# A two-block transformer layer on one core: an eleventh weight buffer, the gate projection moved ahead of the chunk products, and half of the expert loads issued from ScalarE

## The reference, cut to what matters

```python
def second_block(x, mem, ...):
    h = x + _mixer(...)            # differential attention and gated linear attention (GLA), chunks of 64
    h = h + _cross_attention(...)  # queries from h, keys and values from mem_2, 4 heads of 256
    h = h + _hier_moe(...)         # group of 4, then the best 2 of 8 experts in it; 32 experts in all

def expert_block(args):            # for each expert
    hid = jax.nn.silu(xb @ w_gate[e]) * (xb @ w_up[e])   # 1024 -> 512
    return hid @ w_down[e]                               # 512 -> 1024
```

## Time and profile before

| | us |
|---|---|
| median of 3 runs | 1137.18 (1136.93 to 1137.8) |
| profiled execution, its own time | 1140.0 |
| its span, first to last instruction | 1137.7 |
| PE busy | 931.5 (82% of the span) |
| DVE, POOL, ACT busy | 403.1, 243.2, 170.2 |
| q1, the DMA queue with nearly all the bytes (289 MB) | 64.4% of 16 engines' span |

### The profile page before, as it was taken

How to read it: one execution, slowest core, us unless ns; L and a number is a source line. 1 busy time by engine, 2 the same in 40 slices (tenths; PEclk the granted TensorE clock), 3 DMA queues, 4 the chain that set the end, 5 groups by cost and what they waited for, 6 DMA issues and landing times.

```text
span 1137.7 us, 12449 instructions
## 1 busy us (share of the span) xinstructions
PE 931.5 (82%) x5006; PEld 585.4 (51%) x5006; DVE 403.1 (35%) x984; ACT 170.2 (15%) x370; POOL 243.2 (21%) x368
## 2 busy tenths in 40 slices
PE   7999999999999899699999999665656566574837
PEld 3775487789999778575544554221221212131312
DVE  5537834752234827655545524110010101010101
ACT  2113232530001022022312312000000000000000
POOL 4444132043844849630000000000000000000000
PEclk9999999999999999899999999887787878697879
DMA  7636232233545255234228358999999999999997
GB/s 278 199 116 219 96 126 75 75 104 126 195 169 185 77 189 182 74 138 154 78 74 318 131 215 357 429 428 427 429 426 428 427 428 427 430 427 428 428 421 277
DMA packets 64312, 290.38 MB, mean 255 GB/s; under 512 B 9015, under 2 KB 11902, under 8 KB 52222
## 3 DMA queue, kind: packets, MB, share of 16 engines
q1 hardware_dynamic: 63966, 289.04, 64.4%
q10 hardware_dynamic: 288, 0.52, 0.1%
HBM read 288.51 MB, written 1.05 MB: 255 GB/s over the span
## 4 chain that ended last, share of the span: by engine, by line
PE 61%; DMA 27%; DVE 6%; ACT 2%; SPq 2%; issue 1%; ACTq 0%; DVEq 0%
PE ACC L520 11%; PE ACC L661 10%; PE ACC L535 8%; PE AUX L1050 7%; PE ACC L658 7%; DMA ring<-in_w_e_gate_dram 5%; DMA ring<-in_w_e_down_dram 5%; PE ACC L559 5%; DMA SQE<-in_w_e_up_dram 3%; DMA BIG<-in_w_e_up_dram 3%; DMA PJ<-in_w_e_up_dram 3%; DMA PJ<-in_w_e_down_dram 3%; DMA BIG<-in_w_e_gate_dram 3%; PE AUX L1086 2%; PE ACC L942 2%; DMA SQE<-in_w_e_gate_dram 2%
## 5 line engine op out<-in xcount | busy, mean ns | idle before, releaser
L1282 POOL TENSOR_TENSOR ring<-ring 128x256 f32<-128x256 f32 x272 | 200.5, 767 | 190.2 <-PE ACC L661 75.6
L1050 PE MATMUL AUX<-ring,R 128*32 128x512 f32 x416 | 115.9, 721 | 55.0 <-DMA BIG<-in_w_e_up_dram 20.3
L535 PE MATMUL ACC<-BIG,ring 128*128 128x256 f32 (+1 forms) x464 | 106.2, 382 | 0.0
L535 PEld LDWEIGHTS ACC<-BIG,ring 128*128 128x128 f32 (+1 forms) x464 | 84.6, 187 | 15.6 <-issue 3.6
L2282 DVE SCALAR_TENSOR_TENSOR R<-R,AUX 128x512 f32<-128x512 f32 x8 | 5.5, 688 | 233.8 <-ACT R L1660 233.8
L1050 PE MATMUL AUX<-R 128*32 128x512 f32 x112 | 62.9, 726 | 23.3 <-DMA ring<-in_w_e_gate_dram 13.1
L1050 PE MATMUL AUX<-BIG,R 128*32 128x512 f32 x192 | 54.9, 736 | 28.8 <-DMA PJ<-in_w_e_up_dram 21.1
L1050 PEld LDWEIGHTS AUX<-ring,R 128*32 128x32 f32 x416 | 28.6, 129 | 94.7 <-issue 94.7
L520 PE MATMUL ACC<-ring,BIG 128*128 128x512 f32 (+2 forms) x192 | 75.9, 554 | 0.0
L1050 PE MATMUL AUX<-PJ,R 128*32 128x512 f32 x192 | 53.7, 722 | 17.6 <-DMA ring<-in_w_e_up_dram 10.5
L1086 PE MATMUL AUX<-ring,BIG 128*32 128x512 f32 x192 | 52.3, 705 | 13.8 <-DMA BIG<-in_w_e_down_dram 7.4
(11 more groups left out here) (345 smaller groups left out, 1425.0 us busy)
## 6 DMA issues: line engine op xcount, KB each, us to landing
ring<-in_w_in_dram SPq DMA_DIRECT2D x20, 2048.0 KB, 7.8
ring<-in_w_e_gate_dram SPq DMA_DIRECT2D x14, 2048.0 KB, 27.7
ring<-in_w_e_up_dram SPq DMA_DIRECT2D x12, 2048.0 KB, 29.8
ring<-in_w_e_down_dram SPq DMA_DIRECT2D x10, 2048.0 KB, 29.4
BIG<-in_w_e_up_dram SPq DMA_DIRECT2D x8, 2048.0 KB, 32.5
PJ<-in_w_e_gate_dram SPq DMA_DIRECT2D x6, 2048.0 KB, 26.6
BIG<-in_w_e_down_dram SPq DMA_DIRECT2D x6, 2048.0 KB, 29.0
PJ<-in_w_e_down_dram SPq DMA_DIRECT2D x6, 2048.0 KB, 35.2
```

Source lines behind the costliest of these rows:

```text
L535: mm = nc.tensor.matmul(bank[0:m, j * S:(j + 1) * S], w[:, i, a + j * P:a + j * P + m], rhs[:, i, :], start=(i == 0), stop=(i == k - 1))
L1050: mm = nc.tensor.matmul(bank[r, :], M_xt[:, k, r], w[e][:, k, :], start=(k == 0), stop=(k == KD - 1))
L1282: ins = g.tensor_tensor(out[:, k, :], a[:, k, :], b[:, k, :], op)
```

## The change

1. `STREAM` is 11. The new buffer, load 4, is `R12`, which is `R1` and `R2` made one tensor; SP issues it when the turned keys and queries of the cross attention (`xk`, `xq`) are out of it. All later buffers move on by one. To make room, `M_xt` goes to `R4`, `M_o`, `M_gated` and `M_hid` to `GB`, the turned rows for the router (`X3T`) to `BIG2`, the routing scratch over the mask tensors, `OUT` to `PJ`. The `BIG2` load (9) now waits for `("router", 1)`.
2. From load 13 on, the odd ones (39 of them, up to 91) are issued by ACT, behind the tanh, the up products or the down copies of the group that frees the buffer.
3. In the mixer `gg` comes right after `ckv1` on PE, then `kend`, intra, the turns, and the states move into `dv`, after its fourth matmul. On DVE, `gv` is combined whole before `norm_heads`, `ckv1` first thing in its `apply`, then `gg`, `kend`, intra. ACT's tanh of `gg` moves ahead of its drains.
4. Before the mixer, `row_sums` for `mem_2` moves between the two halves of block one's result, and the `rsqrt` for `mem_2` behind `ckv0`; the sums of squares of `X3` get their own columns (76, 77), so that nothing has to wait for those at 64.

```diff
-STREAM = 10
+STREAM = 11
-        stream = [slots[4], slots[5]] + [... ("wcq0", "wcq1")] + spare[0:2] + [
+        stream = [slots[4], slots[5]] + [... ("wcq0", "wcq1")] + [R12[:, :]] + spare[0:2] + [
+        FIRST_BY_ACT, LAST_WHOLE = STREAM + 2, 3 * GROUP * GROUPS - GROUP
+        def by_act(n):
+            return n % 2 == 1 and FIRST_BY_ACT <= n < LAST_WHOLE
# PE
             project_blocks("ckv1", R2T, T_mem2, mem2_sums)
+            project_blocks("gg", XT3, T_x, x1_sums)
             pe.wait_ge(gla_products, 1)
             pe.wait_ge(gla_padded, 1)
+            bank, full = aux(3, "kend")
...
-            project_blocks("gg", XT3, T_x, x1_sums)
-            wait_drained(pe, "kend")
...
-            project("dv", XT3, between=finish_gla)
+            project("dv", XT3, between=finish_gla, after=lambda done, total: make_states() if done == 4 else None)
# SP
-                        if n in (STREAM, STREAM + 1):
+                        if n in (STREAM, STREAM + 1) or by_act(n):
                             continue
                         elif n == 4:
+                            for t in range(TT):
+                                for h in range(2):
+                                    wait_full(sp, ("xk", t, h))
+                                    wait_full(sp, ("xq", t, h))
+                        elif n == 5:
...
                         elif n == 9:
+                            wait_full(sp, ("router", 1))
+                        elif n == 10:
                             wait_full(sp, ("x3", 1, 1))
                             sp.wait_ge(rows_scaled, 2)
# ACT
+            def load_after(g, kind):
+                for e in range(GROUP):
+                    n = load_no(g, kind, e) + STREAM
+                    if by_act(n):
+                        act.dma_start(stream[n % STREAM], weights_of(n)).then_inc(moe_landed[n % STREAM], 16)
             for g in range(GROUPS):
                 act.wait_ge(moe_gate, g + 1)
                 a_.activation(M_gated, AUX[2][:, :], ACT.Tanh, scale=0.5).then_inc(moe_tanh, 1)
+                load_after(g, 0)
+                act.wait_ge(moe_up, g + 1)
+                load_after(g, 1)
                 act.wait_ge(moe_picks_turned, g + 1)
...
+                load_after(g, 2)
# DVE
                 if h == 0:
-                    dve.wait_ge(rows_squared, 4)
-                    rsqrt(2, SMALL[:, 64:66], SMALL[:, 78:80]).then_inc(mem2_scaled, 1)
-            row_sums(T_mem2, quarters(R2T), mem2_sums)
-            norm_rows(3, X3, ZTv, 5)
+                    row_sums(T_mem2, quarters(R2T), mem2_sums)
+            norm_rows(3, X3, ZTv, 5, col=76)
...
-            combine("gv", by_rows(GV), range(1))
+            combine("gv", by_rows(GV))
             def apply_d():
-                combine("gv", by_rows(GV), range(1, 2))
+                combine("ckv1", by_rows(R1v, 512))
...
-            combine("ckv1", by_rows(R1v, 512))
+            combine("gg", by_rows(GG))
             link(v.memset(ATT, 0.0))
```

More of the change, by code:

```diff
@@ L84, in two_block_layer @@
         ident = sb("ident", P)
-        causal = sb("causal", S)
-        past = sb("past", P)
-        future = sb("future", P)
+        MASKS = sb("MASKS", S + 3 * P)
+        causal, past, future, ones = MASKS[:, 0:S], MASKS[:, S:S + P], MASKS[:, S + P:S + 2 * P], MASKS[:, S + 2 * P:]
         before = sb("before", P, BF16)
@@ L831, in _ @@
             project_blocks("ckv1", R2T, T_mem2, mem2_sums)
+            project_blocks("gg", XT3, T_x, x1_sums)
             pe.wait_ge(gla_products, 1)
             pe.wait_ge(gla_padded, 1)
+            bank, full = aux(3, "kend")
+            for t in range(TT):
+                for h in range(2):
+                    mm = nc.tensor.transpose(bank[:, (2 * t + h) * P:(2 * t + h + 1) * P], KE[:, h, t * P:(t + 1) * P],
+                                             ident[:, :])
+            mm.then_inc(full, 1)
             for t in range(TT):
@@ L846, in _, with make_states @@
                 turn(2 + t, ("dk", t))
[L847 to L852, removed]
-            project_blocks("gg", XT3, T_x, x1_sums)
-            wait_drained(pe, "kend")
[L855 to L861, removed]
+            def make_states():
+                wait_drained(pe, "kend")
+                wait_drained(pe, "gv")
+                for c in range(3):
+                    bank, full = aux(c, ("state", c))
+                    for h in range(2):
+                        mm = nc.tensor.matmul(bank[:, h * 256:(h + 1) * 256], KEN[:, c % 2, 2 * (c // 2) + h, :],
+                                              GV[:, c // 2, h * 256:(h + 1) * 256], start=True, stop=True)
+                    mm.then_inc(full, 1)
             def finish_gla():
@@ L954, in score_experts @@
                         wait_drained(pe, ("x3", t, i // 4))
[L955 removed]
+                    mm = nc.tensor.matmul(bank[:, 0:36], X3T[:, i, t * P:(t + 1) * P], WR3[:, i, :],
                                           start=(i == 0), stop=(i == KD - 1))
@@ L1168, in _ @@
             for g in range(GROUPS):
-                for kind, w in enumerate((WG, WU, WD)):
+                for kind in range(3):
                     for e in range(GROUP):
                         n = load_no(g, kind, e)
-                        if n in (STREAM, STREAM + 1):
+                        if n in (STREAM, STREAM + 1) or by_act(n):
                             continue
@@ L1381, in link, with square_rows @@
                 act.wait_ge(act_steps, steps[0])
-            def square_rows(n, src, junk, ready, tiles=range(TT)):
+            def square_rows(n, src, junk, ready, tiles=range(TT), col=64):
                 for r in ready:
@@ L1584, in _ @@
             scale_mem2("ckv1", R1v, 512)
+            act.wait_ge(gla_products, 1)
+            act.wait_ge(gla_padded, 1)
+            wait_drained(act, "gg")
+            a_.activation(R3[:, 0:1024], GG.rearrange("p t n -> p (t n)"), ACT.Tanh, scale=0.5).then_inc(tanh_ready, 1)
             act.wait_ge(pads_cleared, 5)
@@ L2103, in _ @@
             norm_heads(SQ[:, :], 32, 64, apply_d, 2)
-            combine("ckv1", by_rows(R1v, 512))
+            combine("gg", by_rows(GG))
             link(v.memset(ATT, 0.0))
+            bank = wait_full(dve, "kend")
+            kb_ = bank[:, :].rearrange("p (n d) -> p n d", n=4)
+            v.tensor_copy(KEN[0:64, 0, :, :], kb_[0:64])
+            v.tensor_copy(KEN[64:128, 1, :, :], kb_[64:128]).then_inc(free_sem("kend"), 1)
             for t in range(TT):
@@ L2112, in _ @@
                                   pb[:, 1]).then_inc(free_sem(("intra", t)), 1)
-            bank = wait_full(dve, "kend")
-            kb_ = bank[:, :].rearrange("p (n d) -> p n d", n=4)
-            v.tensor_copy(KEN[0:64, 0, :, :], kb_[0:64])
-            v.tensor_copy(KEN[64:128, 1, :, :], kb_[64:128]).then_inc(free_sem("kend"), 1)
-            combine("gg", by_rows(GG))
             for c in range(3):
```

67 lines of the change are left out of this document (33 added, 34 removed).

## The result

The changed kernel takes 1123.47 us (median of 4 runs, 1122.32 to 1124.0), the kernel before, run beside it, 1137.06 (4 runs, 1136.47 to 1137.8). The ratio is 0.9879, 95% interval 0.9862 to 0.9896: faster by 13.6 us. The interval is 11.8 to 15.7 us; the forecast was 17.4 us less, 1119.8, and the range 1113 to 1128. The profiled execution of after took 1124.0 (span 1122.2), that of before 1140.0 (span 1137.7): 16.0 between the two, 15.5 between their spans.

What follows compares the result with a forecast made beforehand. DMA rate bounds the last 430 us, PE the front: the end is the full-queue moment plus bytes left at 428 GB/s. Front 12.5 plus buffer 4.9 is 17.4 us less, median 1119.8, range 1113 to 1128.

Steps and rivals of the forecast that it cites:

- wait before `ckv1`: Mixer: PE's wait for DVE's part 2 of `gv` goes whole, 8.7 us less.
- clock behind it: Mixer: without the wait PE's clock need not fall to half, so `ckv1` is 2.8 us shorter.
- wait before `kend`, clock of `gg`: Mixer: PE's wait for a PSUM bank drained by ACT goes, 2.4 us, and `gg` behind it shortens by 1.0.
- POOL late for `gg`: Mixer: POOL's additions at 0.80 us each finish late, PE waits within `gg`, taking back 3.3 us.
- ahead of the mixer: Before the mixer: DVE's root for x1 starts earlier, shortening PE's 2.88 us wait; 0.9 us less, between 0 and 4.
- eleventh buffer: Its load falls while DMA engines idle, leaving 88 loads instead of 89 at the full queue: 4.9 us less.
- The median of the runs is 2.8 less, and I take the same difference off it: Whole kernel: profiled 1140.0 against median 1137.18; the same 2.8 us was assumed between profile and median after the change.
- Rival 1: Expert stage: two queues fill each other's gaps, rate rises to 434 GB/s, 6 us more gained, 1113.8; chance 0.12.
- rival 4: Expert stage: two queues cost rate; at 406 GB/s 23.2 us more, slower at 1143.0; chance 0.04.
- Rival 3: Change-over to the full queue: a hole eats the extra buffer's lead, 12.5 us gained alone, 1124.7; chance 0.12.
- Rival 2: Front: POOL or DVE slow when packed closer, or the clock drops again; mixer gives 7, 1125.3; chance 0.14.
- in this stretch neither a faster PE nor an earlier issue counts: Expert stage, last 430 us: DMA engines are the bound, each new load standing behind six others.

Runs made afterwards that it cites:

- e7: Kernel before with the eleventh buffer and the moved scratch tensors only, all loads on SP, mixer as before: 1133.18 us, ratio 0.996.
- e3: Changed kernel with ten buffers instead of eleven, `R12` left idle: 1129.38 us, ratio to the kernel before 0.9927.
- e2: Changed kernel with every load issued by SP again: 1124.13 us, ratio to the kernel before 0.9888.
- e8: Changed kernel with every load from 13 on issued by ACT: 1124.56 us, ratio to the kernel before 0.9897.
- e1: Kernel before with only the new order in and ahead of the mixer (parts 3 and 4), ten buffers, all loads on SP: 1129.16 us, ratio 0.9927.
- e4: Changed kernel with POOL's weight sums of `gg` ahead of its three GLA products: 1121.21 us, ratio to the kernel before 0.9854.
- e12: Changed kernel with POOL's `gg` sums first, then the `KE` product, and 9 idle matmuls in the wait for x1: 1120.72 us, ratio to before 0.9858.
- e5: Kernel before, unedited, run again for a second profiled execution: 1136.98 us, ratio 1.0002.
- e10: Kernel before with 12 idle matmuls on PE inside the 2.88 us wait ahead of the turning of x1: 1136.9 us, ratio 1.0.
- e11: Changed kernel with 9 idle matmuls on PE inside the 2.2 us wait ahead of the turning of x1: 1123.55 us, ratio to before 0.9881.
- e6: Kernel before with one edit, DVE combining `gv` whole ahead of `norm_heads`: 1140.48 us, ratio 1.0028.
- e9: Kernel before with 38 idle bf16 matmuls of zeros on PE in the long wait ahead of `ckv1`: 1136.18 us, ratio 0.9989.

## Why the prediction was right, and where it was not

The mechanism was the forecast one: the end is the moment of the full queue plus the bytes left at 428 GB/s, the front moves that moment, and the buffer the bytes. Its terms, from profile to profile:

| term | forecast | measured | from |
|---|---|---|---|
| wait before `ckv1` | 8.7 | 8.7 | no wait in after; part 2 of `gv` on DVE at 458.07, PE asks at 458.80 |
| clock behind it | 2.8 | 2.7 | 14.99 to 12.25 |
| wait before `kend`, clock of `gg` | 3.4 | 3.4 | no wait; the first 3.69 for 16, as at full clock |
| POOL late for `gg` | -3.3 | -5.7 | 471.00 to 488.94 is 17.9, a block is 12.2 |
| ahead of the mixer | 0.9 | 1.0 | `ckv1` begins at 458.80, PE left `gv` at 459.80 |
| rest of the front | 0 | 0.5 | what is left of 10.6 at the router |
| front | 12.5 | 10.6 | router 687.43 to 676.86 |
| eleventh buffer | 4.9 | 4.7 | landing 15.3 earlier, less 10.6; e7 4.5, e3 5.5 |
| issues on ACT | 0 | 0 | no difference shown (e2 1.0, e8 2.0 us slower than after, interval some 2.5); 427 to 428 GB/s |

Two steps failed in size. The first makes up the way from the forecast 17.4 to the 15.3 between the landings (16.0 between the profiled times, 0.5 of it outside the spans), the second the way from there to the 13.6 between the medians.

**POOL's durations.** The step "`gg`'s steps at 475.9, 479.1, 482.3 and 485.5" took 0.80 us an addition from the earlier trace rows. POOL began `gg`'s sums at 471.57, 1.1 earlier than I had it, and PE began `gg` 1.0 earlier; but the twelve additions up to the fifth product took 12.0 us instead of 9.6. In the same stretch DVE's eight scalings of `dq` and `dk` took 8.6 us; in the profile of before, where POOL had nothing to do until 474.96, they took 5.1:

```profile
465.90 1.28 DVE L1751 TENSOR_TENSOR PJ<-PJ,RS 128x512 f32<-128x512 f32 x2
...
468.68 1.29 DVE L1751 TENSOR_TENSOR PJ<-PJ,RS 128x512 f32<-128x512 f32 x2
470.00 2.50 DVE L1757 TENSOR_TENSOR PJ<-PJ,GB 128x512 f32<-128x512 f32 x4
```

The row behind the 0.80 was a mean of two prices. In the profile of before, too, an addition takes 0.73 us as a rule and 1.17 beside the six masked products of the earlier trace rows, which read two operands from SBUF as the scalings do; beside `combine`, whose operations read an accumulator in PSUM, it stays at 0.73:

```profile
L1282 POOL TENSOR_TENSOR ring<-ring x8: 725/728/732, 443.0 to 448.0; 128x256 f32<-128x256 f32 x8
L1282 POOL TENSOR_TENSOR ring<-ring x6: 1052/1173/1258, 448.8 to 454.5; 128x256 f32<-128x256 f32 x6
```

So the price of the two side by side was in the trace of before, and the mean hid it. The new order put the scalings beside the first eight additions of `gg`, and those are what PE waited for: 2.4 us more than the 3.3 of the sum. e1 shows 1.56 and 2.53 us of wait without the buffer and without ACT's issues; e4 and e12 show that the time hangs on POOL's order.

**The step from the profile to the median.** "The median of the runs is 2.8 less, and I take the same difference off it" was wrong. After's profile is only 0.5 above its median, e1's 0.15 below. The profiled execution of before was a long one of its kind, and so was e5's. It carried stretches at half clock that e10's does not have: 1.7 us behind the wait for x1 (2.38 + 4.92 against 1.97 + 3.62), 1.0 in `ckv1` (14.99 against 14.02), and 1.5 from `kend` to the states (14.1 against 12.6). That is 4.2 us, and e10's profiled execution took 1135.8, 4.2 less than before's. After's profile carries the first of the three too, so the pair should differ by 16.0 - 4.2 + 1.7 = 13.5 without them; the medians differ by 13.6. So of the sum's terms "2.8" for the clock behind the wait and "1.0" for `gg` behind `kend`, some 1 us each is there in some executions only. That the median execution of before lacks these stretches is argued, not shown: no profile fell on an unedited execution at 1137, and the match of 13.5 may be luck, for the pair e10 and e11 gives 12.4. What decides whether the clock falls behind a wait of 2 to 3 us also stays open; it fell in before, e5, e7 and after, and not in e1 to e4, e6, e8 and e9, behind waits of 2.2 to 2.9 us.

Rival 1 and rival 4 were about the rate of two queues: it is 427 to 428 GB/s over 100 us in after and in e2, well below rival 1's 434, so both fell. Rival 3 fell with e3 and e7, though its 1124.7 is the nearest number to the result. Rival 2, the mixer gives 7, has its mechanism in the trace: POOL and DVE did get slower when packed closer, at a price of 2.4 us; in the median the mixer gave 8.3, nearer to rival 2 than to the 12.5 of the sum. The change-over cost 0.3 us: load 9 went out at 678.8, at the end of the router product, but the share was full only from 680.6 and not "from about 674". The prediction's "in this stretch neither a faster PE nor an earlier issue counts" held in before and after, but in e4's and e8's profiles PE made the end 1.2 to 1.7 us later. Of what else was priced at nothing, the states' DVE work under four matmuls of `dv` cost nothing that shows.

## What to carry to other kernels

Where transfers end the kernel, two things count first: when the queue is full for good, and how many bytes are still out then; one more buffer was worth one load's time because its load fell into an idle stretch. Look again at the last few us after each gain: in e4 and e8 the products on PE, and no longer the last transfers, were the end. When a reordering puts two engines' work side by side, do not price it with a mean over a long row: split the row by what the other engine did, and take the part in which it did the same. A difference read off one profile should be checked against the spread of the runs: if the profiled execution stands above its median, look for half-clock stretches behind short waits before passing the gain on to the median.

## What the runs showed of the hardware that was not expected

- DVE and POOL side by side slow each other, by what they read: POOL's 128x256 additions take 0.73 us, and 1.17 beside DVE's products of two SBUF operands (before and after); DVE's eight 128x512 scalings take 5.1 us alone and 8.6 beside POOL. Beside the operations of `combine`, which read one operand from PSUM, POOL's additions stay at 0.73.
- The granted clock fell to 0.5 after PE's idle 8.66 us in the long wait, and not when these were filled (e9). After idle stretches of 2.2 to 2.9 us it fell in some executions only, costing 1.7 us where it did.
- Two queues, SP's and ACT's, share 427 to 428 GB/s, the rate of one queue (e2), though unevenly per load: 39.2 us to landing on the one, 27.8 on the other.
